# Two loops turned and one wait moved in the attention stage of a one-core encoder kernel

## The reference

```python
def chunk_rel_attention(q, k, v, rel_table):      # group A
    logits = einsum('bhncd,bhnmd->bhncm', qc, kb) * d ** -0.5   # a chunk of 64 against 9 chunks
    logits = where(band_valid, logits + bias, NEG_INF)
    p = softmax(logits, axis=-1)
    o = einsum('bhncm,bhnmd->bhncd', p, vb)

def swa_sink_attention(q, k, v, t5_table, sinks):   # group B, 2 chunks of keys, 2 key-value heads
    mx = maximum(max(logits), sink)
    e = exp(logits - mx)
    p = e / (sum(e) + exp(sink - mx))
    o = einsum('bkgncm,bknmd->bkgncd', p, vb)
```

## Time and profile before

| what | value |
|---|---|
| median of 3 runs | 3859.51 us |
| lowest and highest | 3855.51 and 3867.56 us |
| the profiled execution's own time | 3859.51 us |
| its span, first to last instruction | 3857.8 us |
| PE busy | 3631.9 us, 94% |
| DVE busy | 1724.7 us, 45% |
| ACT busy | 1645.1 us, 43% |
| mean granted TensorE clock | 0.974 of full speed |

### The profile page before, as it was taken

How to read it: one execution, slowest core, us unless ns; L and a number is a source line. 1 busy time by engine, 2 the same in 40 slices (tenths; PEclk the granted TensorE clock), 3 DMA queues, 4 the chain that set the end, 5 groups by cost and what they waited for, 6 DMA issues and landing times.

```text
span 3857.8 us, 66155 instructions
## 1 busy us (share of the span) xinstructions
PE 3631.9 (94%) x24240; PEld 3247.7 (84%) x24240; DVE 1724.7 (45%) x2452; ACT 1645.1 (43%) x2290; POOL 100.0 (3%) x132
## 2 busy tenths in 40 slices
PE   8999899998999889977999999999999999999993
PEld 5777668886888677747999999999999999999993
DVE  4455433323332433344545555455554544544444
ACT  3455323323332322134546555564654544544542
POOL 1000000000000000010000000000000000000001
PEclk9999999999999999988999999999999999999997
DMA  5111312222222210146666666666565555555446
GB/s 173 34 52 42 115 55 92 92 93 71 93 96 94 104 55 33 55 81 201 193 205 191 206 193 198 201 191 206 191 195 175 164 166 177 164 167 171 158 155 235
DMA packets 150283, 533.85 MB, mean 138 GB/s; under 512 B 17976, under 2 KB 18016, under 8 KB 149936
## 3 DMA queue, kind: packets, MB, share of 16 engines
q1 hardware_dynamic: 126288, 459.86, 36.7%
q0 software_dynamic: 14624, 55.52, 4.0%
q10 hardware_dynamic: 9280, 17.24, 1.5%
HBM read 502.93 MB, written 33.28 MB: 139 GB/s over the span
## 4 chain that ended last, share of the span: by engine, by line
PE 91%; DVE 3%; ACT 2%; DMA 2%; issue 1%; POOL 0%; ACTq 0%; POOLq 0%; DVEq 0%
PE ps L280 29%; PE ps L282 28%; PE ps L281 28%; PE ps L329 1%; PE ps L521 1%; PE ps L506 1%; PE ps L1285 1%; PE ps L460 1%; DMA y<-yrow_d,slot 0%; PE ps L1314 0%; PE ps L541 0%; PE ps L529 0%; PE ps L1079 0%; DVE rstd L311 0%; DMA tok_d<-tokid,slot 0%
## 5 line engine op out<-in xcount | busy, mean ns | idle before, releaser
L275 DVE TENSOR_TENSOR wl<-wraw,wh 128x1024 fp32r<-128x1024 f32 x860 | 1052.1, 1224 | 1558.1 <-ACT wh L271 1558.1
L271 ACT ACTIVATE wh<-wraw 128x1024 fp32r<-128x1024 f32 x860 | 904.4, 1057 | 1197.5 <-PE ps L282 1189.1
L280 PE MATMUL ps<-exh,wh 128*128 128x240 f32 (+3 forms) x3584 | 1021.1, 285 | 11.9 <-issue 9.6
L282 PE MATMUL ps<-exh,wl 128*128 128x240 f32 (+3 forms) x3584 | 1022.2, 285 | 0.0
L281 PE MATMUL ps<-exl,wh 128*128 128x240 f32 (+3 forms) x3584 | 1018.6, 284 | 0.0
L280 PEld LDWEIGHTS ps<-exh,wh 128*128 128x128 f32 x3584 | 679.1, 189 | 12.8 <-issue 12.8
L281 PEld LDWEIGHTS ps<-exl,wh 128*128 128x128 f32 x3584 | 678.4, 189 | 0.0
L282 PEld LDWEIGHTS ps<-exh,wl 128*128 128x128 f32 x3584 | 677.5, 189 | 0.0
L282 PE MATMUL ps<-mah,wl 128*128 (+4 forms) x1792 | 510.5, 285 | 0.0
L280 PE MATMUL ps<-mah,wh 128*128 (+4 forms) x1792 | 509.8, 284 | 0.6
L281 PE MATMUL ps<-mal,wh 128*128 (+4 forms) x1792 | 509.2, 284 | 0.0
(11 more groups left out here) (282 smaller groups left out, 3763.3 us busy)
## 6 DMA issues: line engine op xcount, KB each, us to landing
wraw<-in_w_expert SPq DMA_DIRECT2D x676, 512.0 KB, 3.9
wraw<-in_w_main SPq DMA_DIRECT2D x184, 512.0 KB, 3.2
yrow_d<-yst ACTq DMA_DIRECT2D x16, 512.0 KB
yT<-in_xT POOLq DMA_DIRECT2D x4, 1024.0 KB, 11.3
hT<-in_xT POOLq DMA_DIRECT2D x1, 4096.0 KB, 15.3
h_d<-hT POOLq DMA_DIRECT2D x1, 4096.0 KB, 13.2
hT<-h_d POOLq DMA_DIRECT2D x1, 4096.0 KB, 12.4
xrow_d<-rows ACTq DMA_DIRECT2D x16, 256.0 KB, 2.6
```

The lines of the kernel that those rows point to most:

```text
L271: act.activation(wh[:, j], wraw[:, j], ACT.Copy).then_inc(hi_done, 1)
L275: dve.tensor_tensor(wl[:, j], wraw[:, j], wh[:, j].bitcast(F32), ALU.subtract).then_inc(lo_done, 1)
L280: pe.matmul(out, a_hi, b_hi, start=first, stop=False)
L282: return pe.matmul(out, a_lo, b_hi, start=False, stop=last)
```

## The change

In `attend_pe` the two places with the wait for `sB_y` are replaced by one at the head of the step, ahead of all transposes of group A. The loops of both weighted sums are turned: the head is now outside and the key tile inside, so that all matmuls of head 0 stand ahead of all of head 1. The number of instructions and their data are the same.

```diff
                 if u >= 1:
                     pe.wait_ge(sB_pt, u)
+                    pe.wait_ge(sB_y, u)
                 for kk in range(na):
-                    if u >= 1 and kk == 4:
-                        pe.wait_ge(sB_y, u)
                     for h in range(2):
                         o = T0 + (2 * kk + h) * P
                         mm = pe.transpose(ps[:, o:o + P], eA[:, h, kk * P:kk * P + P], ident[:])
...
                 pe.wait_ge(sA_pt, u + 1)
-                if u >= 1:
-                    pe.wait_ge(sB_y, u)
-                for kk in range(na):
-                    for h in range(2):
+                for h in range(2):
+                    for kk in range(na):
                         v = vA[:, t + 1 - na + kk, (2 * p + h) * HD:(2 * p + h + 1) * HD]
                         mm = pe.matmul(Y_OUT[h * HD:h * HD + HD], v, ptA[:, kk, h], start=kk == 0, stop=kk == na - 1)
...
                 pe.wait_ge(sB_pt, u + 1)
                 pe.wait_ge(sA_y, u + 1)
-                for kk in range(nb):
-                    for h in range(2):
+                for h in range(2):
+                    for kk in range(nb):
                         mm = pe.matmul(Y_OUT[h * HD:h * HD + HD], vB[:, t + 1 - nb + kk, h * HD:h * HD + HD], ptB[:, kk, h],
                                        start=kk == 0, stop=kk == nb - 1)
```

## The result

| | before | after |
|---|---|---|
| time, median (lowest to highest, runs) | 3863.53 us (3855.51 to 3873.75, 6) | 3888.24 us (3885.11 to 3895.32, 6) |
| profiled execution: time, span | 3859.51, 3857.8 us | 3888.9, 3887.3 us |
| attention, first transpose to last sum | 127.2 to 426.4: 299.2 us | 130.0 to 457.4: 327.4 us |

The ratio is 1.0067, interval [1.0052, 1.0082]: the change costs 20 to 32 us. The forecast was 3881, the range 3869 to 3895. In the profiled executions attention is 28.2 us longer. So the time of one execution says little about a few microseconds in attention, and the rows say more.

A forecast was written before the change was run, and what follows sets the result against it. PE, holding 91% of the chain, was taken to bound the kernel, passing delays on unless it would have waited anyway. 10.3 us for the wait plus 11.6 for the turned loops, 21.9 on 3859.51, gave 3881 us, range 3869 to 3895.

The forecast's parts named there:

- The loops: Both weighted sums in attention: turned loops start head 1 later, costing 11.6 us, bounds 0.7 and 24.4.
- head 0's record 2na - 3: Group A's sum: head 1 starts with this record, 0.27, 0.49, 0.70 us late for `na` of 3, 4, 5.
- the reach: Sums on column halves: one half gets past at most three unstarted matmuls of the other, as read from row halves.
- program order: Rival on the sums: head 1 waits for head 0's end, costing 24.4 us, time 3894; chance 0.20.
- the deep look-ahead: Rival on the sums: column halves pass ten matmuls as easily as three, costing 0.7 us, time 3870.5; chance 0.14.
- The upper bound of 24.4: Sums on PE's path: no head 1 record before head 0's last, 158 pairs for group A and 66 for B.
- The wait, what hides it: Moved wait ahead of group A's transposes: cost 0 at `t = 1` and `t = 3`, 0.29 us at `t = 2`.
- My second sign against the forecast: Attention steps: the forecast is wrong if steps of `t = 1` and `t = 3` grow as well.
- The wait, its size: Ahead of group A's transposes: 0.46 us late at `t` of 0, 5, 6, 7, 0.87 at `t = 4`; 10.3 in all.
- some 28 pauses of about 0.4 us: Sign in the profile after: PE idles before group A's transposes (L505), with `ystB` as releaser.
- The clock: PE's granted clock: taken as unchanged, 5 us either side; rival that 4.8 us come back, 3876, chance 0.07.
- the small sums: Some 50 sums in attention with 0.01 us or less of delay each: 0.3 us together.

The follow-up runs named there:

- The blocks: Two runs of the kernel before, with group A's sum alternating heads every two or every three key tiles: 3871.44 and 3866.60 us.
- blocks of two: Kernel before with group A's sum taking two key tiles of head 0, then two of head 1, and so on: 3871.44 us, one run.
- the fourth experiment: Changed kernel with the wait for `sB_y` written ahead of those for `sA_p` and `sB_pt` instead of behind: 3902.98 us, one run.
- blocks of three: Kernel before with group A's sum taking three key tiles of one head, then of the other, then the rest: 3866.60 us, one run.
- the first swapped version: Kernel before with the transposes of `eB` put ahead of group A's sum, the `sB_y` wait staying at the sum: 3859.41 against 3864.43 us, ratio 0.9989.
- the long pause alone: Kernel before with the `sB_y` wait ahead of all transposes only in steps with `t = 4`, elsewhere where it stood: 3875.09 us, ratio 1.0026.

## Why the prediction was right, and where its sizes were off

- **The loops.** Forecast 11.6 us, measured alone 11 us in the median (0.28%) and 3.2 per pair against 3.07. The step that carried it, head 1 starting with head 0's record 2na - 3, holds to 0.01 us for 3, 4 and 5 tiles (0.27, 0.49, 0.70 forecast; 0.27, 0.49, 0.71 measured), and the start of the eighth record with the seventh shows it directly; two tiles cost nothing (0.66). The blocks confirm the reach on column halves, which the trace of before showed for row halves only. With that both rivals on it fall, program order (2.3 or more) and the deep look-ahead (1.34). The upper bound of 24.4 comes out a little too low: counted again by my own rule, the last pair adds 4 more pairs for group A and 13 for group B, which makes 26.3 us. No other term rests on it, but by it the time of program order is 3896 and lies outside my range of 3869 to 3895. By the rule of the Trainium skill, "TensorE: Matmul & The Clock Gate", section "Part 3: Packing small matmuls — row/col tiling", that matmuls start in program order, the sum of five tiles would take 2.3 or more; the measured 2.02, and 1.36 in blocks of two, do not agree with it.
- **The wait, what hides it.** In the third pair `t = 1` costs 0.02, as forecast: the pause for `qAl` turned into one for `ystB`. The slack of `t = 2` is the forecast 0.17 to 0.18, so it costs 0.39 for 0.29, all of it from the size of the delay (next point). `t = 3` was forecast at 0 with a slack of 0.45; its sum of group B starts 5.60 us behind the transposes instead of 5.91, so only 0.31 of 0.57 is hidden and it costs 0.26. My second sign against the forecast named `t = 1` and `t = 3` together; only `t = 3` came, with 0.26 of the 3.8 that the wait costs in the pair.
- **The wait, its size.** This is the term that was mis-sized: 0.46 per exposed step (`t` of 0, 5, 6, 7), measured 0.54 (0.57 at the first transpose; the ten then take 1.28 instead of 1.31, which gives 0.03 back). It rested on the 0.05 between copy and transpose in the earlier trace rows, read off a wait that is attached to the transpose itself. Of three waits, two are in an instruction of their own, and the copy's end then has to pass through that first: 0.15, and 0.05 again once it is written first (the fourth experiment). `t = 4` costs 0.96 for 0.87. Together 4 x 0.54 + 0.02 + 0.39 + 0.26 + 0.96 = 3.8 in the third pair, for 3.00; over attention some 2.5 us. Forecast were also some 28 pauses of about 0.4 us; there are 31, of 0.48 to 0.50 in twenty-four steps and of 1.16 to 1.21 in seven.
- **The clock.** I took no change, on the ground that pauses of 0.49 behind L567 had not lowered it. That ground was right for the 0.5 us pauses and silent on the four of 1.2 us at `t = 4`, a value that my own sum contained (0.87 more than the 0.35 of the earlier trace rows). In after two of the four come with 3.4 us at 0.50, 1.5 us each; in the other kernels up to 10.2 us. On the other side, the last pair lost less than forecast, 3.0 for 3.4 us: the stretch of step 30 is missing there, its sum takes 2.02 at full clock in place of 2.40, and the step is 0.5 shorter instead of 1.1 longer, while steps 27 to 29 grow by 1.7 instead of 1.0. Whether the change gave that clock back is not shown: the stretch is missing from three kernels without the change's wait in that step as well (blocks of three, the first swapped version, the long pause alone), and present with either half of the change.
- **The sum.** In the profiled execution attention grew by 28.2 us for 21.9 forecast. The difference of 6.3: the waits and sums of the first three pairs 20.7 instead of 18.2 (+2.5), two clock stretches at `t = 4` (+3.0), one in step 0, 131.6 to 135.0, which the first swapped version has as well, at 130.5 (+1.5), the last pair (-0.4), and -0.3 for the small sums. Nearly all of it but the 2.5 moves between executions; the medians are 24.7 us apart. Of the 7.2 us between the forecast of 3881 and the measured 3888.24, 4.0 are the base: I started from 3859.51, and the median of before over six runs is 3863.53.

What stays open is why the stretch with `t = 4` is 3.4 us in one execution and 10.2 in another, missing as in step 20 of after, or there without the long pause as in blocks of two; the runs show only that it comes far more often with the pause (10 of 12) than without (1 of 21).

## What to carry to other kernels

When matmuls of two halves of the array are to run beside each other, alternate between the halves in the program at least every two fp32 matmuls; a whole run of one half ahead of the other is paid in full beyond the first three records. A wait that comes last should be attached to the instruction that needs it, or be written first among several. Where PE is otherwise busy, weigh a pause of a microsecond by more than its length: here the wait at the four steps with 1.2 us cost 10.7 us in the medians, of which some 4 are the pauses themselves, and the wait at the twenty-seven others 10.2.

## What the runs showed that I had not expected

- A wait that ends last passes in 0.05 us when the instruction carries it, and in 0.15 us when it stands in an instruction of its own.
- PE's granted clock fell to 0.50 (1.2 GHz) for 3.4 to 10.2 us in or up to 0.8 us behind most pauses of 1.1 to 1.2 us in the first three pairs, where PE is busy for 92% or more of the time, and never behind 24 pauses of 0.5 us in 272.9 us. Once, in blocks of two, it fell with nothing longer than 0.8 us ahead of it.
- The step length at full clock repeats to 0.04 us from pair to pair and from kernel to kernel where the step is not changed, which makes a single profile worth more than ten timed runs for a term of half a microsecond.
